# A transformer kernel on one core: gate and up products of the feed-forward part as 512-column products against a joined high and low activation tile

## The reference

```python
def swiglu(h, w_gu, w_down):                      # layers 0 to 3
    g, u = jnp.split(h @ w_gu, 2, axis=-1)        # 1024 -> 2 x 2816
    return (jax.nn.silu(g) * u) @ w_down          # 2816 -> 1024
...
# layer 4
u = depthwise_conv_centred(hn @ w_up[layer], conv_w[layer], conv_b[layer])   # three taps along the tokens
val, gate = jnp.split(u, 2, axis=-1)
h = h + gate2 * ((jax.nn.silu(gate) * val) @ w_down[layer])
```

## Time and profile before

| | us |
|---|---|
| three runs | 1682.96, 1684.7, 1686.68 |
| median | 1684.7 |
| span of the profiled execution, first to last instruction | 1681.6 |
| PE busy, share of the span | 1593.0, 95% |
| DVE busy | 1213.1, 72% |
| ACT busy | 791.4, 47% |
| mean granted TensorE clock | 0.979 |

### The profile page before, as it was taken

How to read it: one execution, slowest core, us unless ns; L and a number is a source line. 1 busy time by engine, 2 the same in 40 slices (tenths; PEclk the granted TensorE clock), 3 DMA queues, 4 the chain that set the end, 5 groups by cost and what they waited for, 6 DMA issues and landing times.

```text
span 1681.6 us, 30829 instructions
## 1 busy us (share of the span) xinstructions
PE 1593.0 (95%) x12553; PEld 1505.3 (90%) x12553; DVE 1213.1 (72%) x1629; ACT 791.4 (47%) x1042; POOL 86.9 (5%) x105
## 2 busy tenths in 40 slices
PE   2878999999999999999999999979999999999998
PEld 1857999999989999988899999869999989889998
DVE  6897877778368777764487777848777777676665
ACT  3444434356354433554443435545334467654543
POOL 0031000001000000001000000020000002300000
PEclk8988999999999999999999999989999999999999
DMA  9754787855246878563458884514977745345550
GB/s 391 303 217 174 297 315 293 318 181 208 89 193 246 332 306 316 211 221 106 154 216 351 306 310 183 213 76 164 382 302 298 277 156 167 108 173 181 192 175 26
DMA packets 54219, 383.75 MB, mean 228 GB/s; under 512 B 6256, under 2 KB 6512, under 8 KB 8448
## 3 DMA queue, kind: packets, MB, share of 16 engines
q1 hardware_dynamic: 50400, 363.75, 57.4%
q0 software_dynamic: 3744, 18.94, 3.1%
HBM read 378.47 MB, written 4.19 MB: 228 GB/s over the span
## 4 chain that ended last, share of the span: by engine, by line
PE 82%; DVE 10%; DMA 3%; ACT 2%; issue 1%; POOL 1%; SPq 0%; DVEq 0%; ACTq 0%
PE PS L1820 69%; PE PS L1841 4%; DVE wlo L1319 3%; PE PS L1947 2%; DMA CST<-cst_in 1%; DMA adar<-ada 1%; PE PS L1877 1%; PE PS L1973 1%; ACT whi L922 1%; DVE adar L1337 1%; PE PS L1994 1%; DVE NM L1489 1%; DVE XN L1386 1%; DMA raw<-ada 1%; DVE SCR L1483 1%
## 5 line engine op out<-in xcount | busy, mean ns | idle before, releaser
L1820 PE MATMUL PS<-hhi,whi 128*128 128x256 f32 x2536 | 731.9, 289 | 22.7 <-DVE hlo L1379 17.4
L1820 PE MATMUL PS<-hlo,whi 128*128 128x256 f32 x2536 | 724.1, 286 | 0.0
L1820 PE MATMUL PS<-hhi,wlo 128*128 128x256 f32 x2536 | 723.6, 285 | 0.0
L1319 DVE TENSOR_TENSOR wlo<-raw,whi 128x2048 fp32r<-128x2048 f32 x234 | 536.8, 2294 | 250.0 <-ACT whi L922 249.5
L922 ACT ACTIVATE whi<-raw 128x2048 fp32r<-128x2048 f32 x234 | 447.0, 1911 | 479.0 <-PE PS L1820 473.8
L1820 PEld LDWEIGHTS PS<-hhi,whi 128*128 128x128 f32 x2536 | 493.5, 195 | 37.9 <-issue 32.9
L1820 PEld LDWEIGHTS PS<-hlo,whi 128*128 128x128 f32 x2536 | 493.5, 195 | 1.3 <-issue 1.2
L1820 PEld LDWEIGHTS PS<-hhi,wlo 128*128 128x128 f32 x2536 | 493.3, 195 | 0.0
L1337 DVE CUSTOM_DVE_ANT_0 adar<-adar,CB 128x1024 f32<-128x1024 f32 x232 | 276.8, 1233 | 7.9 <-DMA adar<-ada 7.9
L1820 PE MATMUL PS<-ahi,whi 128*128 128x256 f32 x968 | 275.2, 284 | 1.1 <-DVE alo L1770 1.1
L1820 PE MATMUL PS<-alo,whi 128*128 128x256 f32 x968 | 274.6, 284 | 0.0
(11 more groups left out here) (222 smaller groups left out, 1364.6 us busy)
## 6 DMA issues: line engine op xcount, KB each, us to landing
raw<-weights SPq DMA_DIRECT2D x234, 1024.0 KB, 6.4
adar<-ada SPq DMA_DIRECT2D x104, 1024.0 KB, 5.8
adar<-ada POOLq DMA_DIRECT2D x12, 1024.0 KB, 6.5
raw<-ada SPq DMA_DIRECT2D x4, 1024.0 KB, 15.1
bias_rows<-acc POOLq DMA_DIRECT2D x12, 256.0 KB, 3.6
adar<-bias_rows POOLq DMA_DIRECT2D x8, 256.0 KB, 3.2
CST<-cst_in SPq DMA_DIRECT2D x1, 1128.0 KB, 22.7
CB<-c_in SPq DMA_DIRECT2D x2, 512.0 KB, 4.3
```

The costliest lines, as they stand in the source:

```text
L1319: v.tensor_tensor(wlo[:, u % CV, :], raw[:, u % RAW, :], whi[:, u % CV, :].bitcast(F32), ALU.subtract).then_inc(lo_done, 1)
L1820: m = pe.matmul(o, w(a), h(b), start=first and k_ == 0, stop=last and k_ == 2, skip_group_check=True)
```

## The change

- `hhi` and `hlo` become the two halves of one tile, `hboth` (128 x 2 x 8 x 256).
- `wide_product` takes the place of `split_product` for gate and up units: the high weights are multiplied with high and low activations of a chunk in one product of 512 columns, which fills a whole bank, and the low weights with the high activations in a product of 256 columns, which is added in the first half. Each output tile (b, t) has a bank of its own, so a step takes banks 0 to 3, and the last down chunk moves from bank 2 to bank 7 (four zero products instead of five).
- The two halves of a bank are added when they are read: ACT copies the second halves of two banks to `SCR` (`part_copy`), and DVE adds the first halves (`parts_add`). Silu, convolution and product then read `SCR`. `bank_free` waits for these sums.
- `wide_pair` replaces `project_pair` at step 0, without the two zero products.
- The last two chunks of `X` now both wait for the end of the last down unit.
- Down products, mixers and all else keep `split_product`.

```diff
-        hhi = sb("hhi", [P, C, S], F32R)
-        hlo = sb("hlo", [P, C, S], F32R)
+        hboth = sb("hboth", [P, 2, C, S], F32R)
+        hhi, hlo = hboth[:, 0], hboth[:, 1]
...
         def down_bank(c):
-            return bank[4 + c // 2][:, S * (c % 2):S * (c % 2) + S] if c < C - 1 else bank[2][:, 0:S]
+            return bank[4 + c // 2][:, S * (c % 2):S * (c % 2) + S]
+        def ffn_bank(b, t):
+            return bank[2 * b + t]
+        def ffn_part(b, part):
+            return PS[:, 2 * b:2 * b + 2, S * part:S * part + S]
+        def ffn_sum(b):
+            return SCR[:, 4 + b, :]
...
                 def ffn_gate(s_, add=0):
...
-                            act.wait_ge(pe_unit, (f if s_ == 0 else f + 2 + 3 * (s_ - 1)) + h + 1 + 6 * add)
+                            act.wait_ge((g_sum, u_sum)[h], STEPS * l + s_ + 1 + 2 * add)
...
-                        src = bank[0][:]
+                        src = ffn_sum(0)
                     act.activation(SCR[:, 2, :], src, ACT.Silu).then_inc(sg_done, 1)
+                def part_copy(b, s_, add=0):
+                    act.wait_ge(pe_unit, (f if s_ == 0 else f + 2 + 3 * (s_ - 1)) + b + 1 + 6 * add)
+                    if not (isinstance(add, int) and s_ == 0):
+                        act.wait_ge(a32_done, STEPS * l + s_ + 2 * add)
+                    act.activation(two(ffn_sum(b)), ffn_part(b, 1), ACT.Copy).then_inc((g_part, u_part)[b], 1)
...
+                part_copy(0, 0)
+                part_copy(1, 0)
                 hi(f + 2)
                 ffn_gate(0)
                 hi(f + 3)
...
                         hi(f + 4 + 3 * st, add=i)
                         hi(f + 5 + 3 * st, add=i)
-                        ffn_gate(1 + st, add=i)
+                        part_copy(0, 1 + st, add=i)
+                        if kind == "b2":
+                            part_copy(1, 1 + st, add=i)
+                            ffn_gate(1 + st, add=i)
+                        else:
+                            ffn_gate(1 + st, add=i)
+                            part_copy(1, 1 + st, add=i)
                         hi(f + 6 + 3 * st, add=i)
...
+                def parts_add(b, s_, add=0):
+                    v.wait_ge((g_part, u_part)[b], STEPS * l + s_ + 1 + 2 * add)
+                    v.tensor_tensor(two(ffn_sum(b)), ffn_part(b, 0), two(ffn_sum(b)), ALU.add).then_inc((g_sum, u_sum)[b], 1)
                 def ffn_act(s_, add=0):
+                    parts_add(1, s_, add)
...
                 lo(f + 2)
+                parts_add(0, 0)
...
                         lo(f + 5 + 3 * st, add=i)
+                        parts_add(0, 1 + st, add=i)
...
                     if k < 6:
-                        v.wait_ge(y_done, 4 * l + k // 2 + 1)
-                    elif k == 6:
-                        v.wait_ge(y_done, 4 * l + 4)
+                        v.wait_ge(y_done, 3 * l + k // 2 + 1)
                     else:
                         v.wait_ge(pe_unit, f + FFN_UNITS)
...
+                def wide_product(u, b, t, c):
+                    w = slice(UC * c + P * t, UC * c + P * t + P)
+                    o = ffn_bank(b, t)
+                    pe.matmul(two(o), whi[:, u % CV, w], hboth[:, :, c, :], start=c == 0, stop=False, skip_group_check=True)
+                    return pe.matmul(o[:, 0:S], wlo[:, u % CV, w], hhi[:, c, :], start=False, stop=c == C - 1, skip_group_check=True)
...
                 def bank_free(s_, b, add):
-                    if kind == "b2":
-                        pe.wait_ge(cv_vec, 8 * (s_ - 1) + 4 * b + 4 + 16 * add)
-                    else:
-                        pe.wait_ge(sg_done if b == 0 else a32_done, STEPS * l + s_ + 2 * add)
+                    pe.wait_ge((g_sum, u_sum)[b], STEPS * l + s_ + 2 * add)
...
-                project_pair(f, before, 8)
-                for b in (4, 5, 6, 7, 2):
+                wide_pair(f, before, 8)
+                for b in (4, 5, 6, 7):
```

More of the change, by code:

```diff
@@ L241, in program @@
         sg_done, a32_done, ahi_done, alo_done = sem("silu_gate"), sem("act_product"), sem("act_hi"), sem("act_lo")
+        g_part, u_part = sem("gate_low_part_copied"), sem("value_low_part_copied")
+        g_sum, u_sum = sem("gate_parts_added"), sem("value_parts_added")
         cv_act, cv_vec = sem("conv_centre"), sem("conv_sides")
@@ L1037, in mixed_ready @@
                 def mixed_ready(p):
-                    if mixed(kind, p)[0].tensor is hhi[:].tensor:
+                    if mixed(kind, p)[0].tensor is hboth[:].tensor:
                         act.wait_ge(pe_unit, u0 + IN_UNITS[kind])
@@ L1270, in ffn_gate @@
                                 dst = SCR[:, h, 256 * t:256 * t + 256]
-                                e = act.activation(dst, bank[h][:, 256 * t:256 * t + 256], ACT.Identity,
+                                e = act.activation(dst, ffn_sum(h)[:, 256 * t:256 * t + 256], ACT.Identity,
                                                    scale=PAR[:, bass.ds(w + 1 + 32 * add, 1)], bias=PAR[:, bass.ds(w + 3 + 32 * add, 1)])
@@ L1745, in ffn_act @@
                             v.wait_ge(cv_act, 2 * s_ + h + 1 + 4 * add)
-                            b = two(bank[h][:])
+                            b = two(ffn_sum(h))
                             d = two(SCR[:, h, :])
@@ L1759, in ffn_act @@
                     else:
-                        v.wait_ge(pe_unit, (f if s_ == 0 else f + 2 + 3 * (s_ - 1)) + 2 + 6 * add)
-                        val = bank[1][:]
+                        v.wait_ge(u_sum, STEPS * l + s_ + 1 + 2 * add)
+                        val = ffn_sum(1)
                     v.wait_ge(sg_done, STEPS * l + s_ + 1 + 2 * add)
@@ L2182, in half, with wide_pair @@
                     for t in range(2):
-                        o = bank[b][:, S * t:S * t + S]
                         for c in range(C):
-                            m = split_product(o, lambda a: ws[a][:, u % CV, UC * c + P * t:UC * c + P * t + P], lambda x: hs[x][:, c, :], c == 0, c == C - 1)
+                            m = wide_product(u, b, t, c)
                     m.then_inc(pe_unit, 1)
+                def wide_pair(u, before, idle):
+                    full = CST[:].bitcast(BF16)
+                    for _ in range(idle):
+                        pe.matmul(bank[0][:], full[:, 0:P], full[:, 0:512], start=True, stop=True)
+                    unit_ready(u)
+                    unit_ready(u + 1)
+                    for c in range(C):
+                        before(c)
+                        for b in range(2):
+                            for t in range(2):
+                                m = wide_product(u + b, b, t, c)
+                            if c == C - 1:
+                                m.then_inc(pe_unit, 1)
                 def bank_free(s_, b, add):
-                    if kind == "b2":
-                        pe.wait_ge(cv_vec, 8 * (s_ - 1) + 4 * b + 4 + 16 * add)
-                    else:
-                        pe.wait_ge(sg_done if b == 0 else a32_done, STEPS * l + s_ + 2 * add)
+                    pe.wait_ge((g_sum, u_sum)[b], STEPS * l + s_ + 2 * add)
                 def down(u, s_, add=0):
@@ L2203, in down @@
                                               lambda x: acts[x][:, s_ % 2, S * t:S * t + S], False, True)
-                        if s_ == STEPS - 1 and c in (1, 3, 5, 6):
+                        if s_ == STEPS - 1 and c in (1, 3, 5):
                             m.then_inc(y_done, 1)
                     m.then_inc(pe_unit, 1)
-                project_pair(f, before, 8)
-                for b in (4, 5, 6, 7, 2):
+                wide_pair(f, before, 8)
+                for b in (4, 5, 6, 7):
                     pe.matmul(bank[b][:], zeros[:], zeros[:, 0:1].to_broadcast([16, 512]), start=True, stop=True)
```

2 lines of the change are left out of this document (1 added, 1 removed).

## The result

The changed kernel takes 1708.57 us (median of four runs, 1701.6 to 1711.23) against 1685.69 for the kernel before, a ratio of 1.0139 with a 95% interval of 1.0117 to 1.0161: 23 us slower, where 8 were forecast, and above the range of 1675 to 1706.

A forecast was written before the change was run, and what follows sets the result against it. PE's product cost was taken to bound the kernel; -25.0 + 20.3 + 8.8 + 1.8 + 2.2 = +8.1 us on 1684.7 gave 1692.8 us, 8-in-10 range 1675 to 1706.

The forecast's parts named there:

- Product widths: Gate and up units: one 512-column and one 256-column product replace three of 256, saving 14.2 ns each, 25.0 us in all.
- The lower bound, no gain: Gate and up products: 512 columns may cost two times 256, 240.2 ns, nothing saved; as a rival 1717.8 us, chance 0.08.
- the rival of a 216 ns product: Wide gate and up products cost 216 ns, saving 42.6 us; kernel faster at 1675.2 us, chance 0.17.
- The start: Start of each feed-forward part: high part waits behind ACT's copies, step 1 starts 4.4 us later in layers 0-3; 20.3 us together.
- The clock behind the pause: Behind each feed-forward start's pause the granted clock falls, costing 1.75 us in each of five layers, 8.8 us.
- The cover in the loop: Inside the loop, ACT's and DVE's added copies and sums stay hidden behind PE; otherwise up to 1.8 us in each of ten steps.
- The end of layer 4: Ahead of layer 4's last down unit, later gate taps and their sum lengthen the chain, adding 1.8 us.
- The tail of `X`: Both last chunks of `X` now wait for PE's end, 0.45 us in each of five layers, 2.2 us.

The follow-up runs named there:

- e5: e1 without the products of low weights with high activations in gate and up units; time not comparable, undisturbed wide products 226.6 to 226.8 ns apart.
- e1: Changed kernel with the high part of unit f+2 put back ahead of the two copies on ACT; 1673.05 us, ratio 0.9943 to the kernel before.
- e3: Kernel before, with one added wait: ACT makes the high part of unit f+2 only when step 0's up unit is done; 1709.59 us, ratio 1.0165.
- e2: Changed kernel with 20 idle bfloat16 products of 512 columns between step 0's pair and the zero products; 1697.31 us, ratio 1.0078.
- e4: e1 with the chunk loop outside the tile loop in the loop's gate and up units; 1672.46 us in one run.
- e7: e1 with layer 4's gate centre taps ahead of the up copy on ACT and gate outer taps ahead of the up sum on DVE; 1679.26 us, one run.
- e6: e1 with a tile's eight wide products first, then its eight narrow ones, instead of in turn; 1669.06 us, ratio 0.9925.
- e8: e6 and e7 together; 1673.69 us, ratio 0.9948.
- e9: e6 with 13 idle bfloat16 products of 512 columns ahead of layer 4's last down unit; 1669.42 us, ratio 0.9938.

## Why the prediction was wrong, point by point

- **Product widths: the step that failed, by size.** The forecast took 226 ns for the wide product, 120.1 for the narrow one and 25.0 us for all. The wide product by itself is 226.7 ns (e5). In alternation the two cost 353.3 ns in the loops instead of 346.1, and 346.7 only in the pairs and a few units; from a wide product to the next one it is 236 ns there, outside the 221 to 231 that the prediction named as its own test. A loop gains 2.1 us (e1 against before, layers 0 to 3; the same is taken for layer 4) and a pair 0.4: 12.5 us for five layers, half of the forecast. The step went wrong where it added two prices, each read from a row in which products of one length follow each other. The lower bound, no gain, left room for it, and the rival of a 216 ns product is refuted.
- **The start: right.** 5.6 us from the pair's end to the restart were forecast and 5.5 measured; 20.3 us for the five layers, measured 4 x 4.38 + 3.3 = 20.8. In layer 4 the reading was off: the chain's piece that ends at 1493.83 is not the end of the pair, which is at 1494.53, so the pause before was 2.16 us and not 2.86, and 3.3 were added instead of 2.7. e1 and e3 show the cause to be ACT's order, from both sides.
- **The clock behind the pause: right within 2 us.** Forecast 8.8, measured as loop after less loop e1 2.5, 2.3, 2.0 and 2.0 us in layers 0 to 3, and in layer 4 1.9 by the difference that is left there once the wait, the products and the last down unit are taken off, 10.7 together; e2 shows it as a cost of its own. The price of 1.75 us came from one pause of half the length, so that its nearness is in part luck.
- **The cover in the loop: right.** No pause of PE over 0.3 us stands inside a loop of the changed kernel but in layer 4's last step.
- **The end of layer 4: right in kind, half of it missed.** The wait grew by 2.2 us (forecast 1.8). The slower clock behind it, 8.42 - 5.99 = 2.4 us, was not in the sum, though the rule was applied to the other pauses: this one is longer than the 2.36 us of the earlier trace rows and should have been charged the same, though e1 shows that the fall can fail to come.
- **The tail of `X`: right.** 0.3 to 0.4 us a layer, 1.7 in all, forecast 2.2.
- **Not in the sum at all:** at the end of layer 3 PE pauses for 2.6 us with and without the change. In the trace of the changed kernel the clock fell behind it, in that of the kernel before it did not, 1.7 us (13.47 less 11.78, the same stretch in e4, where it did not fall). e1, e2, e3 and e7 have that fall, e4, e6, e8 and e9 have not. It belongs to the scatter of these kernels.

Together: 20.8 - 12.5 + 10.7 + 2.2 + 2.4 + 1.7 + 1.7 - 0.9 = 26.1, as in the spans. Only the clock's term in layer 4 is itself a remainder; the others are read from the traces. Of the 18 us by which the forecast was short of the spans, 12.5 are the products, 4 the clock at the ends of layers 3 and 4, and 2 the clock at the starts; the rest cancels. That the forecast had the sign right owes nothing to the products: with their true saving it would have been +20.6 instead of +8.1.

## What to carry to other kernels

When a change adds instructions to an engine's queue, look first at what stands behind them that needs none of their inputs: here one weight copy behind a wait was dearer than all the products saved. Charge a new pause of PE twice, once for itself and once for the clock behind it, when pauses of its length in the trace at hand are followed by a lower clock; here those of 3 us and more nearly always were. And a price read from a run of equal products holds for equal products; where lengths alternate it has to be measured in alternation.

## What the runs showed of the hardware

- Float32r products in a steady run of equal length lie 120.0 ns apart with 256 columns and 226.7 with 512 (e5). In alternation the two together take 346.7 ns or 353.3; which one can change from unit to unit of the same code, and the loops settled in the slower one in every layer (after, e1, e4). Eight and eight gives 349 (e6). The order of tiles and chunks makes no difference to the loops' time (e4). The cause stays open. The Trainium skill, page "TensorE: Matmul & The Clock Gate", section "Back-to-back issue gap", would give 109.2 and 215.8 ns by its N / 2.4 + 2.5; the trace has 10.8 and 10.9 ns more. The bfloat16 products of 512 columns, 216 ns apart, agree with it.
- At the start of a feed-forward part a pause of PE of 3.1 us (e3, 4.8 in its layer 4) or 4.5 us (after) went each time with 6.8 us at the lower clock level, which began 0.9 to 2.8 us before PE's restart; filled with idle products (e2) with none. In the ten traces of kernels with all their products (e5 is left out), from 160 us on, a stretch at the lower level began between 3 us before and 2 us behind PE's restart in 28 of 29 pauses of 3.0 to 4.8 us, in 5 of 10 of 2.59 us (the end of layer 3), in 9 of 10 of 2.34 to 2.36 us and in 3 of 10 of 2.05 us.
